# Down weights of each expert issued by ScalarE instead of SyncE, in a hybrid mixer and mixture-of-experts block

## What is computed

```python
def expert_block(args):
    xb, e = args
    gu = xb @ w_gate_up[e] + b_gate_up[e]
    gate = jnp.minimum(gu[:, ::2], SWIGLU_LIMIT)
    up = jnp.clip(gu[:, 1::2], -SWIGLU_LIMIT, SWIGLU_LIMIT)
    act = (up + 1.0) * (gate * jax.nn.sigmoid(gate * SWIGLU_ALPHA))
    return act @ w_down[e] + b_down[e]
```

## Time and profile before

| | |
|---|---|
| median of 3 runs | 2252.35 us (2244.6 to 2252.77) |
| the profiled execution | 2252.83 us, span 2251.0 us |
| TensorE matmuls busy | 2038.8 us (91%) |
| VectorE, ScalarE, GpSimd busy | 458.0, 337.9, 194.0 us |
| DMA | 488.57 MB, mean 217 GB/s |
| mean granted TensorE clock | 0.937 |
| the expert stage | from about 1100 to 2207 us, 32 turns |

### The profile page before, as it was taken

How to read it: one execution, slowest core, us unless ns; L and a number is a source line. 1 busy time by engine, 2 the same in 40 slices (tenths; PEclk the granted TensorE clock), 3 DMA queues, 4 the chain that set the end, 5 groups by cost and what they waited for, 6 DMA issues and landing times.

```text
span 2251.0 us, 43117 instructions
## 1 busy us (share of the span) xinstructions
PE 2038.8 (91%) x18196; PEld 959.5 (43%) x18196; DVE 458.0 (20%) x868; ACT 337.9 (15%) x599; POOL 194.0 (9%) x244
## 2 busy tenths in 40 slices
PE   7997797797797799999599999999999999999991
PEld 4455445446446444445234334334344344344340
DVE  1423323323323200032111101101101101011014
ACT  3222222222222200002011001001001001000001
POOL 0001001001001000000211111110110110110110
PEclk9998898898898899998699999999999999999995
DMA  6020010020000522123489999999999999999945
GB/s 231 19 70 11 20 70 10 20 70 10 1 1 1 194 75 75 75 66 157 191 328 388 388 380 392 385 381 396 386 382 398 389 381 393 377 392 392 386 198 202
DMA packets 76306, 488.57 MB, mean 217 GB/s; under 512 B 13636, under 2 KB 14168, under 8 KB 23088
## 3 DMA queue, kind: packets, MB, share of 16 engines
q1 hardware_dynamic: 67536, 470.76, 53.9%
q0 software_dynamic: 8704, 16.82, 2.3%
HBM read 478.53 MB, written 17.45 MB: 220 GB/s over the span
## 4 chain that ended last, share of the span: by engine, by line
PE 88%; DVE 4%; issue 3%; ACT 2%; DMA 1%; DVEq 1%; POOL 0%; ACTq 0%; SPq 0%; POOLq 0%
PE ps L480 32%; PE ps L819 29%; PE ps L837 15%; PE ps L643 2%; DVE arena L1129 2%; DVE arena L1132 1%; PE ps L848 1%; PE ps L804 1%; PE ps L814 1%; ACT arena L888 1%; PE ps L539 1%; PE ps L697 1%; PE ps L663 1%; PE ps L830 1%; PE ps L669 1%
## 5 line engine op out<-in xcount | busy, mean ns | idle before, releaser
L819 PE MATMUL ps<-arena 128*32 128x512 f32 x6144 | 667.7, 594 | 0.0
L480 PE MATMUL ps<-hT,arena 128*128 128x512 f32 x880 | 394.2, 607 | 10.1 <-issue 8.6
L819 PEld LDWEIGHTS ps<-arena 128*32 128x32 f32 x6144 | 184.5, 110 | 465.2 <-issue 459.0
L837 PE MATMUL ps<-arena,hT 128*32 128x256 f32 x6144 | 339.5, 381 | 0.0
L480 PEld LDWEIGHTS ps<-hT,arena 128*128 128x128 f32 x880 | 169.9, 195 | 220.1 <-issue 219.9
L837 PEld LDWEIGHTS ps<-arena,hT 128*32 128x32 f32 x6144 | 185.4, 111 | 142.3 <-issue 2.4
L480 PE MATMUL ps<-arena 128*128 128x512 f32 (+2 forms) x608 | 214.2, 503 | 23.6 <-ACTq L983 16.4
L1534 DVE TENSOR_SCALAR arena<-ps 128x768 f32<-128x768 f32 x32 | 30.6, 957 | 953.1 <-PE ps L819 953.1
L888 ACT ACTIVATE arena<-ps 128x512 f32<-128x512 f32 (+5 forms) x124 | 84.2, 679 | 906.1 <-PE ps L804 697.4
L1630 POOL DMA_INDIRECT expert_rows<-hT,six x96 | 95.7, 997 | 809.5 <-ACT hT L888 762.3
L480 PEld LDWEIGHTS ps<-arena 128*128 128x128 f32 x608 | 112.7, 215 | 107.0 <-issue 74.0
(11 more groups left out here) (201 smaller groups left out, 1111.0 us busy)
## 6 DMA issues: line engine op xcount, KB each, us to landing
arena<-in_w_gu SPq DMA_DIRECT2D x256, 1024.0 KB, 8.1
arena<-in_w_dn SPq DMA_DIRECT2D x128, 1024.0 KB, 6.8
arena<-in_w_pair SPq DMA_DIRECT2D x16, 1024.0 KB, 4.8
arena<-in_w_merge SPq DMA_DIRECT2D x8, 2048.0 KB, 7.7
arena<-expert_rows SPq DMA_DIRECT2D x3, 2048.0 KB, 13.6
arena<-in_x SPq DMA_DIRECT2D x8, 512.0 KB, 10.3
arena<-in_w_out SPq DMA_DIRECT2D x2, 2048.0 KB, 11.2
arena<-in_w_qb SPq DMA_DIRECT2D x4, 768.0 KB, 4.4
```

The lines of the kernel that those rows point to most:

```text
L480: ins = pe.matmul(dst, lhsT, rhs, start=(k == 0), stop=(k == len(pairs) - 1))
L819: ins = pe.matmul(gu[32 * j:32 * (j + 1), g, :], xT[:, k, 32 * g:32 * (g + 1)], ring[k][:, 512 * j:512 * (j + 1)], start=False, stop=(k == ...
L837: ins = pe.matmul(yd[32 * j:32 * (j + 1), g, 0:256], aT[:, g, k, 32 * c:32 * (c + 1)], ring[8 + c][:, D * k + 256 * j:D * k + 256 * (j + 1 ...
```

## The change

The down weights and the down bias of experts 1 to 31 are issued by ScalarE, on its own DMA queue, in each turn between `rows_out(n - 1)` and `act_columns(n)`. SyncE keeps the up weights, the up biases, and the down weights and bias of expert 0. The waits for `dn_used` per chunk remain, except that the bias has none of its own and stands behind them.

```diff
--- before.py
+++ after.py
@@ -396,34 +396,30 @@
                         sp.wait_ge(gu_used, 8 * n + (c + 1 - 8))
                     sp.dma_start(ring[c], w_gu_chunk(e, c)).then_inc(chunk_in[c], 16)
 
-            def down_weights(n, e):
+            def down_weights():
                 for c in range(8, 12):
-                    if not first(n):
-                        sp.wait_ge(dn_used, 4 * n + (c - 7 - 4))
-                    sp.dma_start(ring[c], w_dn_chunk(e, c)).then_inc(chunk_in[c], 16)
+                    sp.dma_start(ring[c], w_dn_chunk(0, c)).then_inc(chunk_in[c], 16)
 
             def up_bias(n, e):
                 if not first(n):
                     sp.wait_ge(gu_used, 8 * n + (1 - 8))
                 sp.dma_start(bcur[0:3, 0:2 * DE], bias_dram[bass.ds(e, 1), :, 0:2 * DE].rearrange("o b f -> (o b) f")).then_inc(bias_gu_in, 16)
 
-            def down_bias(n, e):
-                if not first(n):
-                    sp.wait_ge(dn_used, 4 * n + (1 - 4))
-                sp.dma_start(bcur[0:3, 2 * DE:3 * DE], bias_dram[bass.ds(e, 1), :, 2 * DE:3 * DE].rearrange("o b f -> (o b) f")).then_inc(bias_dn_in, 16)
+            def down_bias():
+                sp.dma_start(bcur[0:3, 2 * DE:3 * DE], bias_dram[0, :, 2 * DE:3 * DE]).then_inc(bias_dn_in, 16)
 
             up_weights(0, 0, range(6))
             sp.wait_ge(bias_st, 48)
             sp.wait_ge(bias_clear, 1)
             sp.wait_ge(filled, MERGE_F.at("yb1", KD // 2 - 1))
             up_bias(0, 0)
-            down_bias(0, 0)
+            down_bias()
             sp.wait_ge(filled, OUT_F.at(f"x{NT - 1}"))
             for t in range(NT):
                 sp.wait_ge(h2_done, t + 1)
                 sp.dma_start(h2_dram[t * P:(t + 1) * P, :], h2[:, t, :]).then_inc(h2_st, 16)
             up_weights(0, 0, range(6, 8))
-            down_weights(0, 0)
+            down_weights()
             sp.wait_ge(table_set, 16 * NT * TOPK)
             for j in range(4):
                 sp.dma_start(tab[32 * j:32 * (j + 1), :], slot_dram.rearrange("(p c) o -> p (c o)", p=32)).then_inc(tab_in, 16)
@@ -432,10 +428,6 @@
             with sp.Fori(2, NE) as e:
                 up_weights(e, e, range(8))
                 up_bias(e, e)
-                down_weights(e - 1, e - 1)
-                down_bias(e - 1, e - 1)
-            down_weights(NE - 1, NE - 1)
-            down_bias(NE - 1, NE - 1)
             sp.wait_ge(list_done, 1)
             extra = sp.value_load(lst[0:1, 2 * LIST:2 * LIST + 1], min_val=0, max_val=MAX_EXTRA)
             with sp.If(extra > 0):
@@ -444,8 +436,6 @@
                         e = sp.value_load(lst[0:1, bass.ds(j + LIST, 1)], min_val=0, max_val=NE - 1)
                         up_weights(j + NE, e, range(8))
                         up_bias(j + NE, e)
-                        down_weights(j + NE, e)
-                        down_bias(j + NE, e)
 
             sp.wait_ge(all_rows, 1)
             sp.dma_start(nrow, norm_final.broadcast_to([P, D])).then_inc(row_in, 16)
@@ -1089,11 +1079,19 @@
                     ac.wait_ge(scattered, 16 * QUADS * n)
                 copy(ys.rearrange("p (g s) -> p g s", g=QUADS), yd[:, :, 0:256]).then_inc(ys_done, 1)
 
+            def down_loads(n, e):
+
+                for c in range(8, 12):
+                    ac.wait_ge(dn_used, 4 * n + (c - 7 - 4))
+                    ac.dma_start(ring[c], w_dn_chunk(e, c)).then_inc(chunk_in[c], 16)
+                ac.dma_start(bcur[0:3, 2 * DE:3 * DE], bias_dram[bass.ds(e, 1), :, 2 * DE:3 * DE].rearrange("o b f -> (o b) f")).then_inc(bias_dn_in, 16)
+
             def expert(n, next_block):
                 if next_block:
                     columns(n + 1)
                 gate(n)
                 rows_out(n - 1)
+                down_loads(n, n)
                 act_columns(n)
 
             ac.wait_ge(list_done, 1)
@@ -1110,6 +1108,8 @@
             with ac.If(extra > 0):
                 with ac.Fori(0, MAX_EXTRA) as j:
                     with ac.If(j < extra):
+                        e = ac.value_load(lst[0:1, bass.ds(j + LIST, 1)], min_val=0, max_val=NE - 1)
+                        down_loads(j + NE, e)
                         columns(j + NE)
                         gate(j + NE)
                         act_columns(j + NE)
```

## The result

The changed kernel takes 2284.89 us (median of 4 runs, 2267.99 to 2287.56), the kernel before on the same chip 2249.69: a ratio of 1.0143, 95% interval 1.0089 to 1.0197. Timed again later it is 1.0121 (1.0082 to 1.016). So it is slower by 1.2 to 1.4%, some 27 to 32 us. The forecast was +12.5 us in a range that reached to +60: the sign was right, the time lies inside the range (2257 to 2312), and the size is more than double.

What follows compares the result with a forecast made beforehand. The prediction took TensorE to pace the expert loop, with the DMA engines nearly full. Its terms 0 + 0 + 3 + 9.5 = +12.5 us on 2252.4 gave 2265 us, with an 8-in-10 range of 2257 to 2312.

Steps and rivals of the forecast that it cites:

- parts 1 and 2: SyncE's lost issues gain nothing (0); ScalarE's added issues, about 2 us between `rows_out` and `act_columns`, are hidden (0).
- Part 3: Expert loop, T0 the end of a `down`: later down loads make the down bias 0.1 us late, 30 turns, +3 us.
- the even sharing: Expert loop: DMA engines serve up and down queues evenly, so 7.1 us of remaining down data takes 14.2.
- Up chunks land by about T0 + 36 and chunk 7 is wanted at T0 + 53: hidden: Expert loop, T0 the end of a `down`: up weight chunks land before `up` wants them, costing nothing.
- 32.9 of 33.89: the total fits: One expert turn: 30.0 us of chunks plus 2.9 of POOL's scatter and gather fit in the 33.89 us turn.
- Part 4: Last expert, no `up` covering its loads: wait before the last `down` about 13 us; +9.5 in all, bounds 7.5 to 12.
- The term for the clock: Last `down`: a lower granted clock after the longer wait costs 0 to 1.5 us more, taken as +1.
- A: Rival, expert loop: not slower, the down bias lands in time, only the last expert costs; 2262 us, chance 0.32.
- B: Rival, expert loop: down bias late every turn by 1 to 2.5 us, 40 to 85 in all; 2307, chance 0.26.
- C: Rival, expert loop: the gather is late for `token_columns` with three queues; 2322, or 2380 with clock loss; chance 0.04.
- D: Rival, expert loop: faster, `down` 0.8 us shorter a turn without load traffic beside it; 2238 us, chance 0.03.

Runs made afterwards that it cites:

- e1_upbias: Changed kernel, but SyncE issues the up bias directly behind up chunk 0 instead of behind chunk 7: 2261.46 us, ratio 1.0049 to the kernel before.
- e4_act_early: Changed kernel, but ScalarE issues the four down chunks ahead of `rows_out`, each behind its own `dn_used`: 2251.65 us, ratio 0.9999 to the kernel before.
- e7_last_early: Changed kernel, with only the last expert's down loads issued ahead of `rows_out`, each chunk behind its own `dn_used`: 2273.41 us, ratio 1.0092 to the kernel before.
- e3_before_bias: Kernel before, SyncE issuing all, with the up bias behind up chunk 0 and the down bias ahead of the down chunks: 2241.53 us, ratio 0.9966.
- e8_before_bias_again: The kernel of e3_before_bias timed again in more rounds: ratio 0.9971 to the kernel before.
- e6_early_bias: e4_act_early with the up bias behind up chunk 0 and the down bias ahead of the down chunks: 2246.1 us, ratio 0.9985 to the kernel before.

## Why the prediction was right and where it failed

**What bounds, and parts 1 and 2: right.** TensorE paced the loop before, and nothing was gained. ScalarE's issues (2.36 us for four) are hidden in the turns. The queues moved as said: SyncE's carries 28% less, about the third that was forecast, and no turn is shorter than 33.88 us.

**Part 3: the transfer looked at was the wrong one, and it came earlier than forecast.** The prediction had the down bias land at T0 + 23.0, where it is wanted at T0 + 23.02, and took +3 us for it. In the changed kernel the last down chunk ahead of it landed at T0 + 19.7 to 21.4, and no turn waited for this bias. In e1_upbias, where nothing else holds the turn, the chunk's median is T0 + 20.8, and the bias was late once in 30 turns, by 0.2 us. So the bias has some 2 us to spare, and the +3 measured nothing. Of the early landing only a part is explained: the first issue was at T0 + 0.4 and not T0 + 0.7, and the even sharing began late. In the turn shown, up chunk 0 was issued at T0 + 5.9 (forecast: T0 + 4.5), and still from 1522 to 1526 the down queue moved 1.18 MB and the up queue 0.12; from 1526 to 1534 it was 1.31 against 1.32 MB, the even shares that the sum assumed.

The cost is elsewhere. The step "Up chunks land by about T0 + 36 and chunk 7 is wanted at T0 + 53: hidden" left out the up bias. It is issued behind chunk 7, lands with it, and is wanted first, at 1539.86 - 1505.12 = T0 + 34.7 (the bias matmuls of the next `up` in the timeline):

```profile
1539.86 0.83 PE L814 MATMUL ps<-arena,ones 128*32 128x512 bf16 x12
```

By the prediction's own numbers the engines start at T0 + 2.0, work 32.9 us and land 1.0 later: T0 + 35.9, that is 1.2 late, or 36 us over 30 turns. Measured are waits of 0.2 to 1.6 on 23 turns, and 21.1 us over the 30 (0.7 a turn) in place of the +3.

The sum "32.9 of 33.89: the total fits" compared the work with the whole turn. The stretch that counts is from the first data of the late issue to the need of whatever is last in the queue: 34.7 less the 2.0 of the start and the 1.0 of the landing, 31.7 us for 32.9 us of work. That the measured time lies inside the range is luck: the range was made wide for a late down bias, which was not late, and the up bias happened to cost what fits into it.

**Part 4: right but for the clock.** Wait 12.94 us (about 13 expected), +8.6 against +8.5. The term for the clock had the wrong sign: +1 was taken, and the last `down` took 11.80 for 13.00, so -1.2 (12.39, so -0.6, in the second profile). The end came to +7.4, a hair under the bounds of 7.5 to 12.

**The rivals.** A (not slower) failed on the up bias; its claim about the down bias was right, and so were its times (T0 + 13 to 22). B came near the size of a turn's wait (its lower end is 1 us, against 0.7) but named the wrong bias. C didn't occur: no transposes wait for `h_rows` in the turns. (Its 2380 doesn't add up either: 30 clock losses of 2.5 us on top of 2322 make 2397.) Its thought that two load queues slow each other is not needed, as e4_act_early shows. D didn't occur: with less load traffic beside it, a `down` of the loop still takes 10.53 us. That no `up` waits for a chunk also came out as forecast.

## What to carry to other kernels

A transfer's slack is counted to the first instruction that wants anything issued at or behind it, not to the use of the large tile: a bias of 12 KB at the end of a queue of 8 MB lands with the last of it and is wanted before the first. Put small operands that are wanted first ahead of the large ones; here the up bias's place removed 21 us from the late kernel, and both places 5 us at the end of the early one. And when loads are, by the estimate, 97% of a turn (32.9 of 33.89), the moment of the first issue counts like bandwidth: moving it behind a whole step opens a hole in the DMA engines that no second queue fills. The loss in the turns takes both, the late issue and the bias at the end of the queue: with early issues (e4_act_early) or with the bias ahead (e1_upbias) it was gone.

## What was not expected

The second hardware queue made no difference to anything that was measured with the issues at the same moments: 1017.78 against 1017.93 us over 30 turns, at a share of 0.99 to 1.00 and 386 GB/s.

The clock came back sooner after the longer wait. It fell from 1.00 (2.4 GHz) to 0.50 (1.2 GHz) some 3 us behind TensorE's last matmul in the kernel before and some 2.5 us in the changed one (0.95 over 2185 to 2186, 0.78 over 2211 to 2212). In the changed kernel it was 0.70 over 2224 to 2226 and 1.00 from 2226, so it was back some 3 us after work began at 2222.09; in the kernel before, after a wait of 4.3 us, it came back only at the end of the window 2191 to 2193, over 5 us after 2187.17:

```profile
2187.20:2189.00 1.80, 1.80 (x24) 1.14 (x28) 0.00 (x0) 0.00 (x0) 0.02 (x1) 0.50 0.08 25
...
2191.00:2193.00 2.00, 2.00 (x24) 0.98 (x20) 0.00 (x0) 0.00 (x0) 0.00 (x0) 0.57 0.00 0
2193.00:2195.00 2.00, 2.00 (x44) 1.18 (x40) 0.00 (x0) 0.00 (x0) 0.00 (x0) 1.00 0.00 0
```

In e7_last_early, after a wait of 4.14 us, it fell only about 5 us behind the last matmul, when TensorE had been at work again for 1 us. Where the wait before the last `down` was about 1 us (e3_before_bias, e8_before_bias_again, e6_early_bias), the clock stayed at 1.00, and the `down` took 11.66 to 11.74 us. In the other runs waits of 2.56 to 12.94 us were followed by a lower clock and 11.80 to 13.07 us, and the longest waits did not bring the longest times. Why is open.
